# Attention in a one-core layer stack: scaling on GpSimd, turning one step later, scores and evacuations in alternation

## The reference, cut to what matters

```python
p_c = masked_softmax(q @ k_cmp, ...)      # compressed keys, about 31 of them
p_s = masked_softmax(q @ k_sel, m_s)      # selected blocks; with 8 blocks and top 16, all of them
p_w = masked_softmax(q @ k_w, m_w)        # window of 512, the whole causal past here
o = gate0 * (p_c @ v_cmp) + gate1 * (p_s @ v_sel) + gate2 * (p_w @ v_w)
```

## Time and profile before

| | |
|---|---|
| median of 3 runs | 2161.75 us (2157.22 to 2166.20) |
| profiled execution, its own time | 2158.83 us |
| its span in the trace | 2157.0 us |
| attention stage in the trace | about 1173 to 1374 us |
| TensorE busy over the span | 2008.3 us, 93% |
| VectorE busy over the span | 757.6 us, 35% |
| GpSimd busy over the span | 263.5 us, 12% |

### The profile page before, as it was taken

The page is one execution under the profiler, slowest core; times in us unless marked ns, Lnnn a source line. Parts: engine busy times, 40 slices in busy tenths (PEclk is TensorE's granted clock), DMA queues, the critical chain, the costliest instruction groups (busy, mean ns, idle before and its releaser), DMA issues. The chain is left out here.

```text
span 2157.0 us, 26506 instructions
## 1 busy us (share of the span) xinstructions
PE 2008.3 (93%) x8626; PEld 1004.3 (47%) x8626; DVE 757.6 (35%) x2018; ACT 401.4 (19%) x880; POOL 263.5 (12%) x253
## 2 busy tenths in 40 slices
PE   8998989999999999977998888998999999999976
PEld 4553554444444444433457555554444444444432
DVE  4692352222222222234111778443222222222216
ACT  2103021111111111100001555211111111111110
POOL 0001100111111111100210000300111111111110
PEclk9999999999999999988998999999999999999998
DMA  7133156999999999879002000216899999999957
GB/s 228 8 62 144 66 220 245 396 417 405 410 397 405 405 395 391 345 293 271 0 0 79 1 1 2 94 49 253 317 407 399 417 408 407 398 413 401 402 222 324
DMA packets 107424, 566.06 MB, mean 262 GB/s; under 512 B 38624, under 2 KB 39392, under 8 KB 69088
## 3 DMA queue, kind: packets, MB, share of 16 engines
q1 hardware_dynamic: 79136, 498.06, 58.2%
q0 software_dynamic: 28224, 67.16, 7.9%
HBM read 539.84 MB, written 59.77 MB: 278 GB/s over the span
## 5 line engine op out<-in xcount | busy, mean ns | idle before, releaser
L438 PE MATMUL moe_bank<-moe_weights,moe_xgT 128*128 128x512 f32 x1024 | 457.0, 599 | 16.7 <-DMA moe_weights<-in_ex_weights 16.3
L438 PEld LDWEIGHTS moe_bank<-moe_weights,moe_xgT 128*128 128x128 f32 x1024 | 189.9, 190 | 233.5 <-issue 215.9
L746 DVE TENSOR_TENSOR moe_hid<-moe_sil,moe_bank 128x256 f32<-128x256 f32 x98 | 41.3, 422 | 659.1 <-ACT moe_sil L621 659.1
L471 PE MATMUL moe_bank<-moe_weights,moe_hidT 128*128 128x512 f32 x512 | 230.5, 593 | 0.0
L441 PE MATMUL moe_bank<-wide,moe_xgT 128*64 128x512 f32 x512 | 226.6, 595 | 0.0
L441 PE MATMUL moe_bank<-moe_weights,moe_xgT 128*64 128x512 f32 x512 | 226.6, 595 | 0.0
L314 POOL DMA_INDIRECT y<-moe_xy,moe_rows x98 | 98.9, 1009 | 945.7 <-DVE moe_idx L726 559.3
L621 ACT ACTIVATE moe_sil<-moe_bank 128x256 f32<-128x256 f32 x98 | 37.6, 383 | 658.6 <-PE moe_bank L438 457.2
L754 DVE TENSOR_SCALAR moe_xy<-moe_bank,moe_sgate 128x512 f32<-128x512 f32 x98 | 73.6, 751 | 219.5 <-PE moe_bank L471 142.1
L471 PEld LDWEIGHTS moe_bank<-moe_weights,moe_hidT 128*128 128x128 f32 x512 | 92.4, 191 | 93.4 <-issue 93.4
L299 POOL DMA_INDIRECT moe_xy<-h,moe_idx x98 | 100.2, 1022 | 267.9 <-DVE moe_idx L726 240.4
(11 more groups left out here) (354 smaller groups left out, 2416.3 us busy)
## 6 DMA issues: line engine op xcount, KB each, us to landing
moe_weights<-in_ex_weights SPq DMA_DIRECT2D x96, 2048.0 KB, 20.7
moe_weights<-in_ex_weights SPq DMA_DIRECT2D x96, 1024.0 KB, 17.9
wide<-in_ex_weights SPq DMA_DIRECT2D x34, 2048.0 KB, 22.4
wide<-in_ex_weights SPq DMA_DIRECT2D x34, 1024.0 KB
moe_weights<-y SPq DMA_DIRECT2D x18, 1024.0 KB, 20.6
wide<-y SPq DMA_DIRECT2D x8, 1024.0 KB, 7.8
moe_xy<-y SPq DMA_DIRECT2D x6, 1024.0 KB, 26.8
oddin_win<-in_od_w_in_heads SPq DMA_DIRECT2D x1, 4288.0 KB, 19.1
```

The costliest lines, as they stand in the source:

```text
L438: mm = pe.matmul(bG[:, :], xgT[:, n, :], wgu[j][:, :, n, :], start=(n == 0), stop=(n == KC - 1))
L471: mm = pe.matmul(bY[half][:, :], hidT[:, n, :], wdn[j][:, n, cols], start=(n == 0), stop=(n == HC - 1))
```

## The change

- There are four `prob` buffers in place of three and three `coef` in place of two.
- The scaling of the four tiles moves from VectorE to GpSimd; VectorE keeps reciprocal and gates.
- TensorE transposes unit k-2 in step k, not unit k-1, and the values follow one step later; the stage has one step more.
- In VectorE's list the copy of hb 1 stands between the masks hb 0, 1 and the masks hb 2, 3. In ScalarE's list the copy of hb 0 stands between the exponentials of hb 0, 1 and those of hb 2, 3.
- In the last head group the query blocks are taken from 3 down to 0.

```diff
-            return n // NT // NU, n // NT % NU, n % NT
+            return n // NT // NU, n // NT % NU, n % NT if n < units - NT else units - 1 - n
...
+        @block.gpsimd
+        def _(pool):
+            for n in range(units):
+                width = (where(n)[2] + 1) * P
+                pool.wait_ge(exp_ready, 4 * n + 4)
+                pool.wait_ge(coef_ready, n + 1)
+                for hb in range(4):
+                    pool.tensor_scalar(prob[n % 4][:, hb, 0:width], prob[n % 4][:, hb, 0:width], coef[n % 3][:, hb:hb + 1], None,
+                                       ALU.mult).then_inc(scaled, 1)
...
-            for k in range(units + 2):
+            for k in range(units + 3):
                 if k + 1 < units:
                     sel_scores(k + 1)
-                if 1 <= k <= units:
-                    turns(k - 1, 0)
-                    turns(k - 1, 1)
+                if 2 <= k <= units + 1:
+                    turns(k - 2, 0)
+                    turns(k - 2, 1)
                     for d in c_turns(k):
                         compressed_turns(d)
                 if k + 1 < units:
                     win_scores(k + 1)
-                if 1 <= k <= units:
-                    turns(k - 1, 2)
-                    turns(k - 1, 3)
-                if k >= 2:
-                    values(k - 2)
+                if 2 <= k <= units + 1:
+                    turns(k - 2, 2)
+                    turns(k - 2, 3)
+                if k >= 3:
+                    values(k - 3)
...
         def _(act):
...
+            for k in range(units + 4):
                 if k < units:
+                    exponentials(k, (0, 1))
+                if 2 <= k <= units + 1:
+                    take_turn(act, copy, k - 2, 0).then_inc(evac_a, 1)
...
+                if k < units:
+                    exponentials(k, (2, 3))
...
+                if 2 <= k <= units + 1:
+                    take_turn(act, copy, k - 2, 2).then_inc(evac_a, 1)
...
-            def scale(n):
+            def coefficients(n):
...
-                dve.wait_ge(coef_ready, n + 1)
-                for hb in range(4):
-                    dve.tensor_scalar(prob[n % 3][:, hb, 0:width], prob[n % 3][:, hb, 0:width], coef[n % 2][:, hb:hb + 1], None,
-                                      ALU.mult).then_inc(scaled, 1)
...
-            for k in range(units + 1):
+            for k in range(units + 2):
                 if k < units:
                     dve.wait_ge(sel_done, k + 1)
-                    if k >= 3:
-                        dve.wait_ge(t_done, turn_of[k - 3, 3] + 1)
+                    if k >= 4:
+                        dve.wait_ge(t_done, turn_of[k - 4, 3] + 1)
                     if k >= 2:
                         dve.wait_ge(exp_ready, 4 * k - 4)
                     mask(k, 0)
                     mask(k, 1)
                     for c, d in enumerate(hosted(k)):
                         compressed_low(d, c)
+                if k >= 2:
+                    take_turn(dve, dve.tensor_copy, k - 2, 1).then_inc(evac_v, 1)
+                if k < units:
                     dve.wait_ge(win_done, k + 1)
                     mask(k, 2)
                     mask(k, 3)
-                if k >= 1:
-                    scale(k - 1)
+                if 1 <= k <= units:
+                    coefficients(k - 1)
                     for d in hosted(k - 1):
                         compressed_scale(d)
-                    take_turn(dve, dve.tensor_copy, k - 1, 1).then_inc(evac_v, 1)
-                    take_turn(dve, dve.tensor_copy, k - 1, 3).then_inc(evac_v, 1)
+                if k >= 2:
+                    take_turn(dve, dve.tensor_copy, k - 2, 3).then_inc(evac_v, 1)
```

More of the change, by code:

```diff
@@ L1781, in attention @@
     with Part(nc, "att") as s:
-        prob = [s.sb(f"prob{p}", [P, 4, SEQ]) for p in range(3)]
+        prob = [s.sb(f"prob{p}", [P, 4, SEQ]) for p in range(4)]
         pT = [s.sb(f"pT{p}", [P, 4, SEQ]) for p in range(2)]
         low, total = [s.sb(f"low{p}", [P, 4]) for p in range(2)], [s.sb(f"total{p}", [P, 4]) for p in range(2)]
-        inv, coef = s.sb("inv", [P, 4]), [s.sb(f"coef{p}", [P, 4]) for p in range(2)]
+        inv, coef = s.sb("inv", [P, 4]), [s.sb(f"coef{p}", [P, 4]) for p in range(3)]
         cp = [s.sb(f"cprob{p}", [P, NT, 2, 32]) for p in range(2)]
@@ L1814, in attention @@
         evacs = []
-        for k in range(1, units + 1):
-            turns = [(k - 1, 0), (k - 1, 1)] + [("c", d) for d in range(8) if max(host(d) + 2, 2 + min(d, 1)) == k] + [(k - 1, 2), (k - 1, 3)]
+        for k in range(2, units + 2):
+            turns = [(k - 2, 0), (k - 2, 1)] + [("c", d) for d in range(8) if max(host(d) + 2, 2 + min(d, 1)) == k] + [(k - 2, 2), (k - 2, 3)]
             for turn in turns:
@@ L1896, in values @@
                                            pT[n % 2][:, 2 * b + half, k * P:(k + 1) * P],
-                                           start=False, stop=(i == NT - 1 and k == i and b == 1))
+                                           start=False, stop=(n % NT == NT - 1 and k == i and b == 1))
                 mm.then_inc(pv_done, 1)
@@ L1911, in _ @@
                     win_scores(k + 1)
-                if 1 <= k <= units:
-                    turns(k - 1, 2)
-                    turns(k - 1, 3)
-                if k >= 2:
-                    values(k - 2)
+                if 2 <= k <= units + 1:
[3 more added lines that the diff above has]
+                    values(k - 3)
         def take_turn(eng, copy, n, hb):
-            turn, width = turn_of[n, hb], (n % NT + 1) * P
+            turn, width = turn_of[n, hb], (where(n)[2] + 1) * P
             eng.wait_ge(t_done, turn + 1)
@@ L1928, in _, with exponentials @@
             copy = lambda out, in_: act.activation(out, in_, ACT.Copy)
-            for k in range(units + 3):
-                if k < units:
-                    for hb in range(4):
[L1932 to L1943, removed]
+            def exponentials(k, hbs):
+                for hb in hbs:
+                    width = (where(k)[2] + 1) * P
+                    act.wait_ge(masked, 4 * k + hb + 1)
+                    if k >= 2 and hb == 0:
+                        act.wait_ge(coef_ready, k - 1)
+                    act.activation(prob[k % 4][:, hb, 0:width], prob[k % 4][:, hb, 0:width], ACT.Exp, scale=-1.0,
+                                   bias=low[k % 2][:, hb:hb + 1], accum_out=total[k % 2][:, hb:hb + 1]).then_inc(exp_ready, 1)
+            for k in range(units + 4):
+                if k < units:
+                    exponentials(k, (0, 1))
+                if 2 <= k <= units + 1:
+                    take_turn(act, copy, k - 2, 0).then_inc(evac_a, 1)
                     for d in c_turns(k):
@@ L1949, in _ @@
                         copy(cpT[d % 2][:, :], bT[turn % 2][0:64, :]).then_inc(evac_a, 1)
-                    take_turn(act, copy, k - 1, 2).then_inc(evac_a, 1)
-                if k >= 6 and k % NT == 2:
+                if k < units:
+                    exponentials(k, (2, 3))
+                    for d in hosted(k):
+                        act.wait_ge(c_shifted, d + 1)
+                        flat = cp[d % 2][:].rearrange("p i h n -> p (i h n)")
+                        act.activation(flat, flat, ACT.Exp, scale=-1.0).then_inc(c_exp, 1)
+                if 2 <= k <= units + 1:
+                    take_turn(act, copy, k - 2, 2).then_inc(evac_a, 1)
+                if k >= 7 and k % NT == 3:
                     d = k // NT - 1
@@ L1959, in mask @@
             def mask(n, hb):
-                i, width = n % NT, (n % NT + 1) * P
+                i, width = where(n)[2], (where(n)[2] + 1) * P
                 bank, half = (bSel, bWin)[hb // 2], hb % 2
-                dve.tensor_tensor_reduce(prob[n % 3][:, hb, 0:width], bank[:, half, 0:width], g.c["causal"][:, (NT - 1 - i) * P:NT * P],
+                dve.tensor_tensor_reduce(prob[n % 4][:, hb, 0:width], bank[:, half, 0:width], g.c["causal"][:, (NT - 1 - i) * P:NT * P],
                                          1.0, 3e38, ALU.add, ALU.min, low[n % 2][:, hb:hb + 1]).then_inc(masked, 1)
@@ L1996, in scale @@
                 dve.wait_ge(inv_ready, n + 1)
-                dve.tensor_tensor(coef[n % 2][:].rearrange("p (b a) -> p b a", a=2), inv[:].rearrange("p (b a) -> p b a", a=2),
+                if n >= 3:
+                    dve.wait_ge(scaled, 4 * n - 8)
+                dve.tensor_tensor(coef[n % 3][:].rearrange("p (b a) -> p b a", a=2), inv[:].rearrange("p (b a) -> p b a", a=2),
                                   gates[:, i, pair, :, j, 1:3].rearrange("p a b -> p b a"), ALU.mult).then_inc(coef_ready, 1)
-                dve.wait_ge(coef_ready, n + 1)
-                for hb in range(4):
-                    dve.tensor_scalar(prob[n % 3][:, hb, 0:width], prob[n % 3][:, hb, 0:width], coef[n % 2][:, hb:hb + 1], None,
-                                      ALU.mult).then_inc(scaled, 1)
```

7 lines of the change are left out of this document (3 added, 4 removed).

## The result

The changed kernel takes 2199.2 us (median of 4 runs, 2196.6 to 2202.3) against 2163.6 for the kernel before: a ratio of 1.0175, 95% interval 1.0154 to 1.0196. It is slower by 36 us, clear of the scatter of either kernel; I had forecast 2172, with 2157 to 2198 as range. The profiled execution took 2196.6 us, 37.8 more than the one of before.

What follows compares the result with a forecast made beforehand. A chain through VectorE and TensorE in turn, neither engine's load, bounds the stage. Terms +9.4 + 0.2 + 2.1 - 1, plus 0.8 for the clock, give +11.5: 2170 or 2173, forecast 2172, range 2157 to 2198.

Steps and rivals of the forecast that it cites:

- The series: VectorE and TensorE lists: masks, scores, transposes and copies all wait in turn; 25.1 us a head group against 23.5.
- The clock term: Whole kernel: half of one more fall of TensorE's granted clock, 0.8 us added to the sum.
- the rival, priced at 2208: TensorE's work in shorter pieces lowers its clock half of the time: +38 us, 2208; chance 0.08.
- GpSimd: Scalings on GpSimd: 0.75 us at 512 columns, 1.64 as upper end, hidden; no hold on VectorE taken.
- 3.3 us of slack: Between the end of a unit's coefficients and TensorE's need of its first scaled tile: 3.3 us, hiding even 1.64 us scalings.
- The sign that I had named: TensorE waiting for GpSimd at its transposes would show the forecast wrong.
- The end: From the masks of unit 28 to the stage's last copy: 31.4 us against 29.3, +2.1.
- The three steps: Steps 28, 29 and 30, with masks 512, 384 and 256 wide: 7.2, 6.9 and 6.0 us.
- The start: Units 0 to 3 of the stage: -1 us, bounds -3 and +3.
- The fast rival: Lists overlap, VectorE loses 5 us a head group and nothing new is in series: about 19 us each, 2130; chance 0.12.

Runs made afterwards that it cites:

- the kernel with one gap filled: Changed kernel, TensorE repeating the selected scores five times only in the step with 512-wide masks, while it would wait for masks: 2177.7 us, ratio 1.0077.
- the filled one: Changed kernel, TensorE repeating the selected scores 5, 2, 2, 1 times for widths 128 to 512 while it would wait for masks: 2172.4 us, ratio 1.0063.
- the kernel with masks together: Changed kernel with VectorE's copy of hb 1 moved behind masks hb 2, 3, all scalings still on GpSimd: 2153.3 us, ratio 0.9965.

## Why the prediction was wrong

- **The series** was right, in kind and size. I summed 25.1 us a head group; at full clock it is 24.9 (the kernel with one gap filled). Single steps: 6.8 and 5.7 us measured for the masks of 256 and 384, in the changed kernel too, which the terms give as 6.8 and 5.9; 6.9 and 6.0 for units 29 and 30, predicted 6.9 and 6.0. With the clock up, units 4 to 28 lie 150.9 us apart in the kernel with one gap filled, for a predicted 150.
- **The clock term failed**: "half of one more clock dip (0.8)". What it measured: the changed kernel spends 176.3 us from unit 4 to unit 28, the filled one 152.4, so 24 us there, and 4 more after it (37.1 against 33.2); its start is 2 us shorter. Over the whole profiled execution 24.5 us come back (2196.6 against 2172.1). I had the rival, priced at 2208, and gave it 0.08, because the idle stretches "are 1 to 2 us, no longer than now". That premise was wrong. The kernel before has one idle stretch of TensorE over 1 us in a head group, 1.35 us (1.48 in the last before unit 28), and lost the clock once in 143 us, at one of these. The new order has three, 1.73, 1.07 and 1.47 us, each ahead of the window scores, and loses the clock at the longest of them in every head group. The range ended 1 us under the measured time because it left this rival out.
- **GpSimd** was mis-sized by two (1.56 at 512 for 0.75), with next to no effect: 3.3 us of slack covered it, as the text said even 1.64 would be. The sign that I had named, a wait for GpSimd at the transposes, did appear, as 14 us of weight loads in 240; the matmuls themselves wait 0.3 us. In the kernel with masks together, where the slack is used up, it is 29 and 12. That it doesn't hold up masks and copies was right.
- **The end** was predicted at 31.4 from unit 28 on; 33.2 with full clock, 37.1 without. The three steps were right (7.2, 6.9, 6.0); the part behind the masks of unit 31 was 1.8 us too short. The start was 1.9 shorter for a predicted 1.
- **The fast rival** (2130) needed masks 2, 3 ahead of copy 1. That alone gives 2153; its number was neared (2140) by a kernel that also puts the coefficients ahead of copy 1 and splits the scalings.

Open: why one run of steps keeps its clock and the next loses it. The filled kernels show that matmuls in the gap of 1.73 us are enough to keep the clock in the regular groups, not that such a gap always costs it. With scalings on VectorE and the same gap in every head group, the mean clock was 0.78 in the first groups and 0.94 in the last, and after the gap of 1.74 us ahead of unit 28 it didn't fall at all.

## What to carry to other kernels

When two engines each work through a list in order, write both lists beside each other with their waits, and look for the path in which every item is in series: moving work off the busier engine wins nothing if the move also puts a wait between two items that used to stand together. A new gap on TensorE can have a second price, here 7 to 14 us at half the clock in each head group. Compare the new gaps with the longest one of the kernel before, one by one; where they are longer, don't price the clock at nothing, and test it by filling the gap with matmuls that change no result. If the granted clock comes back and the kernel gets faster with more work, it was the clock. Gaps in every step alone don't cost it: with masks together and VectorE scaling there are gaps of 1.33 and 1.43 us in each head group at a clock of 1.00.

## What the runs showed of the hardware that I had not expected

- Five extra score pairs (1.1 us of repeated matmuls in a head group of 25) held the granted clock at 1.00 for 100 us; without them it fell to 0.50 once in every head group, and the step of the 128-wide masks went from 5.8 us to 8.3 to 9.6.
- A GpSimd scaling by a per-row factor, f32 in place: 0.615 us at 128 columns, 0.922 at 256, 1.242 at 384, 1.564 at 512: 0.3 fixed and 2.5 ns a column, against 0.482 in all for 512 on VectorE.
- VectorE's scalings, two back to back beside GpSimd's: 0.70 on average in place of 0.48 at 512; with a copy between the two, 0.48 again beside GpSimd's. Its 4-column coefficients beside GpSimd's: 0.30 in place of 0.165 on average, 0.66 in the longest seen.
